# Token mixer of a two-block transformer kernel: pooling and all queries ahead of the attention, half output projections as filler in its steps

## The reference

```python
def token_mixer(h, ...):                       # h: 512 x 1024
    z = h @ w_in                               # 1280 wide: u 512, q 512, k 128, v 128
    # pooling: 4 groups of 128 columns, windows 2, 4, 8, 16
    d_g = mean(u_g over the last w_g tokens) - u_g
    pool_out = (d_g @ w_pool[g]) * pool_scale
    q, k = partial_rope(q), partial_rope(k)
    # 8 heads of 64, 2 key heads, blocks of 128 queries against the 256 keys before and in them,
    # banded mask, softmax with a sink in the denominator
    attn_out = swa_with_sinks(q, k, v, sinks)
    y = concat([rms_norm(pool_out, g_pool), rms_norm(attn_out, g_attn)])
    return y @ w_out                           # 1024 x 1024
x = x + rms_norm(token_mixer(rms_norm(x, mix_pre), ...), mix_post)
```

## Time and profile before

| | us |
|---|---|
| median of 3 runs (lowest, highest) | 2230.09 (2225.47, 2234.53) |
| profiled execution | 2226.57 |
| its span | 2224.7 |
| PE busy in it | 2160.7 |
| DVE busy in it | 1256.1 |
| ACT busy in it | 823.8 |
| POOL busy in it | 195.5 |

### The profile page before, as it was taken

The page is one execution under the profiler, slowest core; times in us unless marked ns, Lnnn a source line. Parts: engine busy times, 40 slices in busy tenths (PEclk is TensorE's granted clock), DMA queues, the critical chain, the costliest instruction groups (busy, mean ns, idle before and its releaser), DMA issues.

```text
span 2224.7 us, 34776 instructions
## 1 busy us (share of the span) xinstructions
PE 2160.7 (97%) x14168; PEld 1800.5 (81%) x14168; DVE 1256.1 (56%) x1889; ACT 823.8 (37%) x1312; POOL 195.5 (9%) x142
## 2 busy tenths in 40 slices
PE   6999999999999999999999999999999899999998
PEld 5877788787888888888888888888896588888887
DVE  4789988898755554444533554443247835444423
ACT  4345443345444333232322532332243544222222
POOL 0100222103323001000000100000000210000000
PEclk9999999999999999999999999999999999999999
DMA  4242111121112243332332323333221112323321
GB/s 161 79 133 76 58 44 44 54 77 63 39 39 77 88 154 115 103 95 94 107 104 83 105 77 98 99 94 117 91 66 57 39 58 75 94 95 101 115 92 51
DMA packets 56171, 189.89 MB, mean 85 GB/s; under 512 B 6256, under 2 KB 8688, under 8 KB 56048
## 3 DMA queue, kind: packets, MB, share of 16 engines
q1 hardware_dynamic: 53168, 182.88, 25.6%
q10 hardware_dynamic: 2880, 5.24, 0.6%
HBM read 178.66 MB, written 9.44 MB: 85 GB/s over the span
## 4 chain that ended last, share of the span: by engine, by line
PE 80%; issue 9%; DVE 7%; ACT 2%; POOL 0%; DMA 0%; SPq 0%; ACTq 0%; DVEq 0%; POOLq 0%
PE pg L655 68%; PE pC L915 4%; PE pB L915 1%; DVE cpad L1884 1%; DVE sacc L2026 1%; DVE w_lo L1804 1%; PE pB L686 1%; ACT w_hi L1223 1%; PE pA L975 1%; PE pC L759 1%; PE pB L693 0%; PE pA L733 0%; PE pB L717 0%; PE pC L733 0%; DVE a_lo L1863 0%
## 5 line engine op out<-in xcount | busy, mean ns | idle before, releaser
L655 PE MATMUL pg<-a_hi,w_hi 128*128 128x512 f32 (+1 forms) x1920 | 746.9, 389 | 12.0 <-ACT ptile L1313 3.9
L655 PE MATMUL pg<-a_lo,w_hi 128*128 128x512 f32 (+1 forms) x1920 | 739.7, 385 | 0.0
L655 PE MATMUL pg<-a_hi,w_lo 128*128 128x512 f32 (+1 forms) x1920 | 737.5, 384 | 0.0
L1804 DVE TENSOR_TENSOR w_lo<-w_raw,w_hi 128x1024 fp32r<-128x1024 f32 (+3 forms) x299 | 382.5, 1279 | 390.2 <-ACT w_hi L1223 389.4
L1223 ACT ACTIVATE w_hi<-w_raw 128x1024 fp32r<-128x1024 f32 (+3 forms) x299 | 329.6, 1103 | 646.6 <-PE pg L655 635.7
L655 PEld LDWEIGHTS pg<-a_hi,w_hi 128*128 128x128 f32 x1920 | 362.9, 189 | 86.7 <-issue 8.0
L655 PEld LDWEIGHTS pg<-a_hi,w_lo 128*128 128x128 f32 x1920 | 362.6, 189 | 68.8 <-issue 1.6
L655 PEld LDWEIGHTS pg<-a_lo,w_hi 128*128 128x128 f32 x1920 | 362.9, 189 | 67.4 <-issue 0.9
L655 PE MATMUL pg<-h_hi,w_hi 128*128 128x512 f32 (+1 forms) x572 | 215.6, 377 | 0.6 <-DVE w_lo L1804 0.6
L655 PE MATMUL pg<-h_hi,w_lo 128*128 128x512 f32 (+1 forms) x572 | 214.5, 375 | 0.0
L655 PE MATMUL pg<-h_lo,w_hi 128*128 128x512 f32 (+1 forms) x572 | 212.4, 371 | 0.0
(11 more groups left out here) (360 smaller groups left out, 2332.4 us busy)
## 6 DMA issues: line engine op xcount, KB each, us to landing
w_raw<-in_w_gu SPq DMA_DIRECT2D x132, 512.0 KB, 3.5
w_raw<-in_w_in SPq DMA_DIRECT2D x74, 512.0 KB, 3.5
w_raw<-in_w_dn SPq DMA_DIRECT2D x48, 704.0 KB, 4.1
spill_g<-tmp ACTq DMA_DIRECT2D x16, 256.0 KB, 2.0
w_raw<-in_w_co SPq DMA_DIRECT2D x8, 512.0 KB, 4.0
w_raw<-in_w_do SPq DMA_DIRECT2D x8, 512.0 KB, 3.9
w_raw<-in_w_wo SPq DMA_DIRECT2D x8, 512.0 KB, 3.9
w_raw<-in_w_pg SPq DMA_DIRECT2D x8, 512.0 KB, 3.6
```

Of the source, the lines that this page charges most:

```text
L655: ins = pe.matmul(dst[:, cols], w_of(w, n % 2, k), b(k)[:, cols], start=first and q == 0, stop=last and q == len(todo) - 1)
L1804: dve.tensor_tensor(w_lo[:, n % 2, 0:c], w_raw[:, n % 4, 0:c], w_hi[:, n % 2, 0:c].bitcast(F32), ALU.subtract).then_inc(S("w_lo"), 1)
```

## The change

All four pooling inputs and all four queries now come before the attention, with window sums, pooling products, the pooling half's norm and its scaling. The output projection of units 0 to 5 is split: the half over the four pooling tiles (`mp`, 12 products) needs no attention output, the half over the four attention tiles (`ma`, 12 products) does. The four first pooling halves are the filler in the steps, 2 products in steps 2 to 15 and 6, 7, 7 in the three closing ones; the fifth and sixth stand around the attention half's norm. ACT copies each pooling half out into free tiles (`pool_out`), DVE adds it to the attention half. The scale mix_post is now put on where x is updated. Units 6 and 7 stay whole.

```diff
-        MIX = [("mk", 0), ("mv", 0), ("mq", 0), ("mq", 1), ("mq", 2), ("mu", 3), ("mq", 3),
-               ("mu", 2), ("mu", 1), ("mu", 0)]
-        MFILL = MIX[5:]
+        MIX = [("mk", 0), ("mv", 0), ("mu", 3), ("mu", 2), ("mu", 1), ("mu", 0), ("mq", 0), ("mq", 1),
+               ("mq", 2), ("mq", 3)]
+        HALF_K = KT // 2
+        MFILL = [(("mp", t), 3 * HALF_K) for t in range(4)]
+        MSTEP = [0] * 2 + [2] * 14 + [6, 7, 7]
...
-        for i in range(KT):
+        for nm, k0 in (("mp", 0), ("ma", HALF_K)):
+            for i in range(KT - 2):
+                U.add((nm, i), a["w_out2"][i][:, k0 * P:(k0 + HALF_K) * P], HALF_K * P)
+        for i in range(KT - 2, KT):
             U.add(("mo", i), a["w_out2"][i], KT * P)
...
+        MAUX = {1: 3, 2: 4}
+        YP = {("mu", 1): 3, ("mu", 0): 2, ("mq", 0): 1, ("mq", 1): 0}
+        for key in MIX:
             O.add(key, "D")
+            if key in YP:
+                aux(("yp", YP[key]), "A")
...
+            def half_unit(key, k0, part=None):
+
+                n = U.at[key]
+                if part is None or part[0] == 0:
+                    pe.wait_ge(S("w_lo"), n + 1)
+                    begin(key)
+                ins = products(n, act_a(k0), HALF_K, bank(key), w_tile, part, ready=("a_lo", set_count("out", k0)))
+                if part is None or part[1] == 3 * HALF_K:
+                    ins.then_inc(S("gemm"), 1)
...
-            unit(("mq", 0))
-            unit(("mq", 1), part=(0, NORM_AT))
+            unit(("mu", 3), part=(0, NORM_AT))
             rotate(0)
...
+            unit(("mu", 3), part=(NORM_AT, UNIT))
+            unit(("mu", 2))
+            unit(("mu", 1))
+            pooled(3)
+            unit(("mu", 0))
+            pooled(2)
+            unit(("mq", 0))
+            pooled(1)
+            unit(("mq", 1), part=(0, NORM_AT))
+            rotate(1)
+            pooled(0)
             unit(("mq", 1), part=(NORM_AT, UNIT))
             unit(("mq", 2), part=(0, NORM_AT))
-            rotate(1)
+            rotate(2)
+            norm(6)
             unit(("mq", 2), part=(NORM_AT, UNIT))
+            unit(("mq", 3), part=(0, NORM_AT))
+            norm_out(6)
+            unit(("mq", 3), part=(NORM_AT, UNIT))
...
-                if s < 15:
-                    unit(MFILL[s // 3], part=(s % 3 * UNIT // 3, (s % 3 + 1) * UNIT // 3))
-                if s == 0:
-                    rotate(2)
-                for k in MAUX.get(s, []):
-                    (rotate if k[0] == "rp" else pooled)(k[1])
-            pooled(0)
-
-            norm(6)
-            norm_out(6)
+                if s in MAUX:
+                    rotate(MAUX[s])
+                for key, q, e, n in mixer_parts(s):
+                    half_unit(key, 0, (q, e))
+
+            half_unit(("mp", 4), 0, (0, 8))
             norm(7)
+            half_unit(("mp", 4), 0, (8, 12))
+            half_unit(("mp", 5), 0, (0, 4))
             norm_out(7)
+            half_unit(("mp", 5), 0, (4, 12))
             for t in range(KT - 2):
-                unit(("mo", t), ready=None if t else fresh("out"))
+                half_unit(("ma", t), HALF_K)
...
+            def pool_half(t):
+                after(("mp", t))
+                act.activation(pool_out(t), bank(("mp", t)), ACT.Copy).then_inc(S("evA"), 1)
...
+                if s == 15:
+                    act.activation(ost[:, 0:1], ost[:, 0:1], ACT.Sqrt)
+            act.wait_ge(S("oat"), PT_)
+            square(7, PT_ - 1, mo[:, KT - 1])
+            pool_half(3)
             root(7)
...
-                unit_out(act, ("mo", t))
-                full_square(2, t, bank(("mo", t)))
-                act.activation(hb2[:, t], bank(("mo", t)), ACT.Copy, scale=v("mix_post", t)).then_inc(S("evA"), 1)
-                after(("mo", t))
+                after(("ma", t))
+                ev_wait(act, ("ma", t))
+                full_square(2, t, hb2[:, t])
...
+            mixed(("mq", 2))
+            rotated(2)
+            recip(6, (1,), dst=tmp2)
+            for t in range(PT_):
+                scaled_out(t, 50, tmp2[:])
+            mixed(("mq", 3))
...
+                if s in MAUX:
+                    rotated(MAUX[s])
+                if s < PT_:
+                    low("out", s, mo[:, s])
...
+            after(("mp", 3))
+            recip(7, (0,))
+            after(("mp", 4))
+            recip(7, (1,))
+            for t in range(PT_, KT + 1):
+                if t < KT:
+                    scaled_out(t, 50, rstd[:])
+                if t == PT_ + 2:
+                    after(("mp", 5))
+                if t > PT_:
+                    low("out", t - 1, mo[:, t - 1])
             for t in range(KT - 2):
-                after(("mo", t))
+                unit_out(dve, ("ma", t))
+                dve.tensor_tensor(hb2[:, t], bank(("ma", t)), pool_out(t), ALU.add).then_inc(S("evD"), 1)
+                after(("ma", t))
             half_recip(2, 0)
-            new_x(2, hb2, 1.0, "ffn2_pre", {
+            new_x(2, hb2, "mix_post", "ffn2_pre", {
```

More of the change, by code:

```diff
@@ L540, in filled, with mixer_parts, mixer_done, pool_out @@
             return [key for key, q, e in parts(R, g) if e == UNIT]
+        def mixer_parts(s):
+            q, end, at_ = sum(MSTEP[:s]), sum(MSTEP[:s + 1]), 0
+            for key, n in MFILL:
+                if max(q, at_) < min(end, at_ + n):
+                    yield key, max(q, at_) - at_, min(end, at_ + n) - at_, n
+                at_ += n
+        def mixer_done(s):
+            return [key for key, q, e, n in mixer_parts(s) if e == n]
+        def pool_out(t):
+            return wd[:, t] if t < PT_ else up[:, t - PT_, PW:]
         tmps = (tmp1, tmp2)
@@ L1166, in turn @@
                     pe.wait_ge(S("qk2"), 2)
+                if s < 2:
+                    pe.wait_ge(S("rstd"), 7)
                 wait(pe, "ptcp", s - 1)
@@ L1711, in _, with pooled @@
             ffn("1", 4, "ffn1_post", None, "mix", "mix_pre")
+            def pooled(g):
+                aux_out(act, ("yp", g))
+                act.activation(mo[:, g], bank(("yp", g)), ACT.Copy, scale=gate_p[:, 46 + g:47 + g])\
+                    .then_inc(S("evA"), 1)
+                ev_wait(act, ("yp", g))
+                square(6, PT_ - 1 - g, mo[:, g])
             after(("mk", 0))
             after(("mv", 0))
-            after(("mq", 0))
             act.wait_ge(S("vtp"), 1)
             act.activation(vt2[:], quad(pc2[:, 0], NB), ACT.Copy).then_inc(S("vtc"), 1)
-            after(("mq", 1))
-            after(("mq", 2))
+            for key in MIX[2:]:
+                if key == ("mq", 1):
+                    pooled(0)
+                after(key)
+                if key in YP and key != ("mq", 1):
+                    pooled(YP[key])
+                if key == ("mq", 1):
+                    root(6)
             def prob(s):
@@ L1748, in _ @@
                     pt_copy(s - 2)
[L1749 to L1765 removed]
+                for key in mixer_done(s - 1) if s else []:
+                    pool_half(key[1])
+                if s in (7, 11, 15):
+                    i = (s - 7) // 4
+                    act.wait_ge(S("oat"), i + 1)
+                    square(7, i, mo[:, PT_ + i])
+                if s == 15:
[3 more added lines that the diff above has]
+            pool_half(3)
+            root(7)
+            pool_half(4)
+            high_out(PT_)
+            high_out(PT_ + 1)
+            pool_half(5)
+            high_out(PT_ + 2)
+            high_out(PT_ + 3)
             for t in range(KT - 2):
[L1767 to L1770 removed]
+                after(("ma", t))
+                ev_wait(act, ("ma", t))
+                full_square(2, t, hb2[:, t])
             def taken_late(t, h):
```

117 lines of the change are left out of this document (46 added, 71 removed).

## The result

The changed kernel takes 2237.26 us in the median of 20 runs (2233.36 to 2243.64), the kernel before 2232.64 in runs on the same chip. The ratio is 1.0031, 95% interval 1.0021 to 1.0041: slower by 4.7 to 9.2 us, inside 0.5%. The two medians alone stand 4.6 us apart, a ratio of 1.0021. The forecast, 2235.0 against a median of 2230.09, is a ratio of 1.0022.

The account below looks back on a forecast made before the run. TensorE, 97% busy, bounds the kernel before; VectorE paces the steps after. At full clock 148.7 us replace 146.2, +2.5; clock and locked ports add 2.5: +5.0, so 2231.6 profiled and 2235 median, range 2223 to 2249.

Parts of the forecast that it names:

- (1): Input units and pooling ahead of the attention: TensorE sum 48.4 us, third query unit ending at 1724.3.
- (2): VectorE's row before the first step: 8.9 us, first step at 1733.2, TensorE through about 1730.8.
- (3): Attention steps to step 15's bias: VectorE's work 47.3 us plus 4 for imperfect feeding, 51.3 in all.
- DVE sets the pace: In the steps the bound moves to VectorE: 2.63 us a step against TensorE's 2.55.
- (4): TensorE behind the last bias: 9.1 us, then 8.5 for half units five, six and the norm, through at 1802.1.
- (5): Attention halves: first 1.3 us late, further triples 2.0 more, 16.3 of products, 2.9 half unit; end at 1824.6.
- (6): Clock fall in the early steps, 1 to 2 us, and VectorE locked beside GpSimd, about 1; +2.5 for both.
- Clock 1.00 behind the steps: Sign for the forecast: the clock is 1.00 behind the attention steps.
- The waits go: Rival: waits go and nothing replaces them, TensorE stays the bound, nearly all 23 us return, 2210; chance 0.12.
- The clock keeps falling: Rival: clock falls repeatedly inside the steps; with eight or nine of sixteen, +19 us, 2254; chance 0.15.
- a low clock through several steps: Sign that the forecast is wrong: the clock stays low through several attention steps; no size given.
- Without its small losses: Rival: same shift of bound, VectorE fed without gaps (-4), first attention half not late (-3), 2228; chance 0.08.

Follow-up runs that it names:

- e1: Changed kernel with the four pooling scalings and the high parts of these activations moved into steps 0 to 3; ratio 1.0029 to the kernel before.
- e7: Changed kernel with the attention norm's sums and spreading behind both pooling halves (fifth and sixth), without cover; ratio 1.0035 to the kernel before.
- e5: Changed kernel with VectorE's low weight halves (w_lo) of the output projections one step later; ratio 1.0020 to the kernel before.
- e3: Changed kernel with the normalising multiplications cut to one column of a head's block, for measuring only; ratio 1.0015 to the kernel before.
- e2: Changed kernel without filler products in steps 0 to 15, their 28 products moved to the last three steps; ratio 1.0069 to the kernel before.
- g1: Changed kernel with late w_lo, fourth query's products six a step in steps 0 to 3, rotations and activations spread; 2224.10 us, ratio 0.9962 to the kernel before.
- g2: g1 with both rotations in steps 4 and 5 and four pooling-half products in each of steps 7 to 18; ratio 0.9985 to the kernel before.
- h1: Changed kernel with the fourth query's 24 products as filler in steps 1 to 5, pooling halves in steps 8 to 18; ratio 1.0029 to the kernel before.
- e4: Kernel before with the normalising multiplications cut to one column of a head's block, for measuring only; ratio 1.0001 to the kernel before.
- e6: Changed kernel with the edits of e3 and e5 together; ratio 0.9996 to the kernel before.
- g3: e5 with the 48 pooling-half products spread forward, 10 instead of 20 in the last three steps; ratio 1.0018 to the kernel before.

## Why the prediction was right

**(1) In front of the attention** the forecast had TensorE through with the fourth query 54.9 us from the mark; it took 55.2 (scores at 1735.56). The wait for a bank between second and third query unit was 0.88 for an expected 1.0.

**(2) VectorE before the first step**: mask at 57.3 forecast, 57.6 measured. The forecast had TensorE through 2.4 us ahead of this point; by e1 the margin is 1 us.

**(3) The steps** were forecast at 51.3 at the full clock. They took 52.95 with the 1.6 of a low clock that e7 prices, so 51.35 otherwise; e7 itself has 51.35. VectorE was busy for 87% and TensorE for 74%, for some 90 and 70 forecast. The parts differ: VectorE was busy for 45.8 where 47.3 were given, and idle for 7.1 (5.6 in e7) where 4 were given; 2.2 of the idle time are w_lo behind ScalarE's w_hi, a wait that my sum didn't have (e5). The sentence "DVE sets the pace" was only half right. e3 took 4.3 us of its work away for 0.3, though e2 took 6.3 us of TensorE's products away and most steps stayed as long to 0.03 us. What turns is a ring: scores, bias, exponential, normalising, transposes, copy, values and filler, through three engines that each work in program order. The right term was VectorE's sum plus its waits, and that I had its size is in part luck, two errors of 1.5 against each other. VectorE's steps 1 to 3, the part without waits, were forecast at 5.2, 5.3 and 3.3 and took 5.03, 5.16 and 3.23.

**(4), (5) Behind the steps**: bias to first attention half forecast 18.9, measured 20.0 (1790.99 to 1811.00). The step is right, the size short, in part at least by the clock: behind the 3.35 us wait for step 14's probabilities TensorE had half its rate from 1792.0 to 1795.4, and four transposes took 1.12 for 0.60. The halves to the last output unit took 21.9 for 21.2; the wait of 0.6 us for its weights, part of the 146.2 before, has gone as forecast.

**(6) Clock and lock** (VectorE held up beside GpSimd) were given 2.5. 1.6 are seen for one stretch in the steps and 1.0 for the lock; two more stretches of 3.4 us stand behind the steps (1792.0 to 1795.4 and 1812.4 to 1815.8), in which (4) and (5) overran by 1.8 together, and no run prices them apart. "Clock 1.00 behind the steps" was wrong: 0.91.

**The sum.** 57.3 + 51.3 + 18.9 + 21.2 + 2.5 = 151.2 forecast, 57.6 + 52.95 + 20.0 + 21.9 = 152.5 measured, for 146.2 before. +5.0 was forecast and +6.2 measured in the profiles; the ratio's 4.7 to 9.2 hold both.

**The rivals.** *The waits go*: both norms' did, and the ones on probabilities took their place as said. *The clock keeps falling*: in the steps it fell twice, behind waits of 2.8 and 3.0 us, for 10.2 of the 53 us, and stayed at 1.00 where the waits were at most 1.1 (until the one of 3.35 that begins at 1788.6, in the last of these us):
```profile
1757.80:1791.00 33.20, 26.20 (x152) 14.71 (x152) 28.45 (x89) 18.47 (x66) 1.28 (x1) 1.00 0.06 15
```
By the Trainium skill ("TensorE: Matmul & The Clock Gate", section on the second HAM failure mode, PSUM-queue depth-cycling) frequent short idles swing the clock; these 33 us, with TensorE busy for 79% and a small wait in most steps, don't agree. But e2 had one fall in the same part of the steps, where its waits were at most 1.6 us, and the changed kernel one at 1812.4, behind waits of 1.2 and 0.9. So long waits are not the only place of a fall:
```profile
1776.60:1780.00 3.40, 3.40 (x14) 1.57 (x14) 3.17 (x7) 1.06 (x6) 1.04 (x1) 0.53 0.00 0
```
In their first steps e1 and e2 had the clock low for 17.1 us on end, so falls that last do occur there; the lengths of e2's steps show no price for it, since VectorE paces them. A sign that was to speak against the forecast, a low clock through several steps, did come (steps 1, 2, 4 and 5), but at a price of 1.6 us. *Without its small losses*: VectorE's idle time was above the 4 it was given, and the first attention half waited 1.2 for a_lo where 1.3 were given.

## What to carry to other kernels

When filler leaves a pipelined loop, add up each engine's program order per step, and then look for instructions in it that wait for the last instruction of another engine's step. Of two such waits (w_lo on w_hi, 1.1 us each) one cost its full length and the other nearly nothing; setting w_lo a step later brought the last bias 2.0 us forward, 0.6 of it by moving a w_lo behind it. An edit of the filler also moves what hangs on it: with e2's products the w_lo left the steps, too. Put filler and side work one piece a step, into the steps where the pacing engine has its short turn: with the same 24 products added, the steps grew by 8 us when VectorE's side work was piled on two steps, and by 0.5 when it was spread and w_lo set a step later (2.5 against the kernel that had the late w_lo already).

## What the hardware showed that was not expected

**The clock falls elsewhere too.** In code that none of these kernels changes, stretches of 20 us show 1.00 before and 0.91 after, with TensorE busy throughout (before, then after):
```profile
740.00:760.00 20.00, 20.00 (x121) 17.69 (x121) 12.81 (x20) 7.68 (x11) 0.00 (x0) 1.00 0.45 144
```
```profile
740.00:760.00 20.00, 20.00 (x117) 17.70 (x116) 8.98 (x14) 5.81 (x8) 0.00 (x0) 0.91 0.24 79
```
This one put the changed kernel 1.6 us back. e1, e2, e5 and e7 show 0.91 in the same stretch too, g1, g2 and h1 0.83, and e3, e4, e6 and g3 1.00. Another 2.7 us of its 4.5 arose in the first 130 us. g1's profiled execution had lost 9.6 us before the mixer, against the profile of before, and its median is still the lowest. A single profile of this kernel compares nothing below 10 us unless it is counted from a mark near the change.

**VectorE beside GpSimd.** Two normalising multiplications of 128x256, 0.62 us elsewhere, took 1.58 while a GpSimd addition ran (VectorE, then GpSimd, changed kernel):
```profile
1779.70 1.58 DVE L2568 TENSOR_SCALAR sm<-sm,sml 128x256 f32<-128x256 f32 x2
```
```profile
1779.60 1.28 POOL L2617 TENSOR_TENSOR acc<-acc,sq 128x512 f32<-128x512 f32 x1 [63.72 <-ACT sq L1288]
```
The addition ended at 1780.88, and the pair 0.40 us later: nearly a full stop of VectorE until it ends. The Trainium skill ("SBUF — State Buffer", section "SBUF: two separate sides") states that the two engines' shared port pair is locked for a whole instruction and not split, against VectorE operations in a two-port mode or with two inputs from SBUF; the trace agrees with a lock, with 1.0 us lost, and no run here shows the multiplications' mode.
